# A two-layer hybrid block: rounded weights' products first, ada pieces moved, GLA roots by ScalarE, mLSTM chain ahead of a low part

## The reference, cut to what matters

```python
for layer in range(DEPTH):
    mod = (silu(c) @ ada_w[layer] + ada_b[layer])[:, None, :]
    sh_m, sc_m, g_m, sh_f, sc_f, g_f = jnp.split(mod, 6, axis=-1)
    h = rms_norm(x, norm_w[layer, 0]) * (1.0 + sc_m) + sh_m
    y = even_mixer(h, ...) if layer % 2 == 0 else odd_mixer(h, ...)
    x = x + g_m * rms_norm(y, norm_w[layer, 1])
    h = rms_norm(x, norm_w[layer, 2]) * (1.0 + sc_f) + sh_f
    y = conv_ffn(h, ffn_in_w[layer], ffn_conv_w[layer], ffn_conv_b[layer], ffn_out_w[layer])
    x = x + g_f * rms_norm(y, norm_w[layer, 3])

def odd_mixer(h, w_in, a_w2, a_b, g_norm_w, w_out):
    ...
    o = rms_norm(gla(...), g_norm_w.reshape(G_HEADS, G_DV))
    return (o * silu(gr)).reshape(b, t, -1) @ w_out
```

## Time and profile before

| | us |
|---|---|
| median of three runs | 2381.96 (2379.38 to 2383.01) |
| the profiled execution | 2381.75 |
| its span, first to last instruction | 2379.7 |
| TensorE busy | 2336.1 (98%) |
| VectorE busy | 2001.0 (84%) |
| ScalarE busy | 1052.4 (44%) |
| DMA, mean over the span | 263 GB/s |

### The profile page before, as it was taken

The page is one execution under the profiler, slowest core; times in us unless marked ns, Lnnn a source line. Parts: engine busy times, 40 slices in busy tenths (PEclk is TensorE's granted clock), DMA queues, the critical chain, the costliest instruction groups (busy, mean ns, idle before and its releaser), DMA issues.

```text
span 2379.7 us, 32710 instructions
## 1 busy us (share of the span) xinstructions
PE 2336.1 (98%) x12512; PEld 2005.1 (84%) x12512; DVE 2001.0 (84%) x2821; ACT 1052.4 (44%) x1181; POOL 15.8 (1%) x22
## 2 busy tenths in 40 slices
PE   8999999999999999999999999999999999999998
PEld 7789898788878888888888888888888888888886
DVE  7779998999989999999888778888887688877875
ACT  2144545544434444344465554655434343433343
POOL 0000010000000000000000000000000000000000
PEclk9999999999999999999999999999999999999999
DMA  9999977677799778977848545385556755576553
GB/s 393 413 395 370 378 260 284 245 257 260 263 376 348 265 257 299 395 261 259 330 181 314 198 171 184 142 338 192 180 191 225 288 198 189 194 275 233 182 194 142
DMA packets 114766, 625.73 MB, mean 263 GB/s; under 512 B 12801, under 2 KB 13249, under 8 KB 63441
## 3 DMA queue, kind: packets, MB, share of 16 engines
q1 hardware_dynamic: 113938, 619.81, 70.1%
q10 hardware_dynamic: 704, 4.23, 0.5%
HBM read 621.85 MB, written 2.13 MB: 262 GB/s over the span
## 4 chain that ended last, share of the span: by engine, by line
PE 79%; DVE 10%; DMA 7%; ACT 3%; issue 1%; DVEq 0%; ACTq 0%
PE bank L2152 32%; PE bank L2154 17%; PE bank L2179 8%; PE bank L2181 8%; PE bank L2180 8%; DMA region<-ada_pieces 5%; DVE lo L1132 4%; DMA piece<-ada_pieces 1%; DVE region L1155 1%; ACT hi L644 1%; PE bank L2149 1%; PE bank L2150 1%; DVE piece L1155 1%; PE bank L2058 1%; PE bank L1908 0%
## 5 line engine op out<-in xcount | busy, mean ns | idle before, releaser
L2152 PE MATMUL bank<-act,hi 128*128 128x512 f32 x3328 | 1048.2, 396 | 4.3 <-DVE act L1217 2.9
L644 ACT ACTIVATE hi<-raw 128x2048 fp32r<-128x2048 f32 x375 | 717.9, 1914 | 753.3 <-PE bank L2181 387.6
L1132 DVE TENSOR_TENSOR lo<-raw,hi 128x2048 fp32r<-128x2048 f32 x375 | 857.6, 2287 | 128.2 <-ACT hi L644 127.7
L2154 PEld LDWEIGHTS bank<-act,lo 128*128 128x128 f32 x3616 | 670.0, 188 | 147.5
L2154 PE MATMUL bank<-act,lo 128*128 128x256 f32 x3616 | 711.9, 278 | 0.0
L2152 PEld LDWEIGHTS bank<-act,hi 128*128 128x128 f32 x3328 | 506.9, 189 | 6.5 <-DVE act L1217 3.3
L2179 PE MATMUL bank<-hi,mid 128*128 128x512 f32 x704 | 274.9, 391 | 1.6 <-DVE lo L1132 1.6
L2180 PE MATMUL bank<-lo,mid 128*128 128x512 f32 x704 | 274.0, 389 | 0.0
L2181 PE MATMUL bank<-hi,mid 128*128 128x512 f32 x704 | 274.0, 389 | 0.0
L1155 DVE SCALAR_TENSOR_TENSOR piece<-piece,cond 128x1024 f32<-128x1024 f32 x207 | 250.8, 1218 | 12.4 <-DMA piece<-ada_pieces 12.3
L2179 PE MATMUL bank<-hi,act 128*128 128x512 f32 x512 | 203.5, 398 | 5.5 <-DVE lo L1132 4.5
(11 more groups left out here) (215 smaller groups left out, 1834.5 us busy)
## 6 DMA issues: line engine op xcount, KB each, us to landing
raw<-w_units SPq DMA_DIRECT2D x378, 1024.0 KB, 4.8
piece<-ada_pieces SPq DMA_DIRECT2D x207, 512.0 KB, 5.6
region<-ada_pieces SPq DMA_DIRECT2D x137, 512.0 KB, 8.0
raw<-head_units SPq DMA_DIRECT2D x16, 1024.0 KB, 16.0
y<-ada_pieces SPq DMA_DIRECT2D x30, 512.0 KB, 6.7
extra<-ada_pieces SPq DMA_DIRECT2D x10, 512.0 KB, 5.8
region<-gamma_scratch ACTq DMA_DIRECT2D x4, 1024.0 KB, 7.4
x<-x_in SPq DMA_DIRECT2D x2, 1024.0 KB, 6.1
```

The lines of the kernel that those rows point to most:

```text
L644: sc.activation(hi[:, slot, :], raw[:, raw_slot, :], ACT.Copy).then_inc(s_hi, 1)
L1132: ve.tensor_tensor(lo[:, slot, :], raw[:, raw_slot, :], hi[:, slot, :].bitcast(F32), ALU.subtract).then_inc(s_lo, 1)
L2152: pe.matmul(both, w, act[:, k, :], start=k == 0, stop=False)
L2154: i_ = pe.matmul(dst, w, act[:, k, 0:T], start=False, stop=k == DK - 1)
```

## The change

- TensorE waits for `hi` before a unit and forms all its products with the high part of the weight first; then it waits for `lo` (`rest_ready`) and forms the others. In a phase's last unit, which is summed block by block, this holds for each block.
- In the mLSTM columns VectorE runs `after_split` (the head chain) ahead of the next unit's low part.
- In the norm the low part of the phase's second unit goes behind the last two activation parts (`low(6)`, `low(7)`).
- Ada pieces move: (2, 2, 2, 2) to (1, 2, 2, 3) in the mLSTM columns, two pieces from layer 0's second ff_down to layer 1's mixed phase.
- GLA: ScalarE takes the inverse root by `Ln` and `Exp(-0.5 x)` from the bank; VectorE's mean and reciprocal are gone. A root that loads ScalarE's table for the norm is also taken in mixed phases, at unit 6.

```diff
--- before
+++ after
@@ -110,19 +110,19 @@
               Phase("values", 0, 1, 8, (3, 2) * 4, side="fox", side0=2, ring=EARLY),
-              Phase("columns", 0, 2, 4, (2,) * 4, dest=MO, side="mlstm"),
+              Phase("columns", 0, 2, 4, (1, 2, 2, 3), dest=MO, side="mlstm"),
               Phase("mixed", 0, 1, 16, (0, 0, 0, 1, 1, 2, 2, 2, 1, 2, 2, 2, 2, 1, 1, 0), ring=(0, 1, ROWS)),
...
               Phase("ff_up", 0, 8, 4, (1, 1, 1, 0), 1, ring=(0, 1, GAMMA)),
-              Phase("ff_down", 0, 1, 16, (2, 2, 2, 2, 2, 3, 2, 2, 2, 2, 2, 2, 2, 2, 2, 2), 1, ring=(0, 1, GAMMA, GAMMA + 1)),
+              Phase("ff_down", 0, 1, 16, (2,) * 15 + (1,), 1, ring=(0, 1, GAMMA, GAMMA + 1)),
               Phase("ff_up", 0, 6, 4, (1, 1, 1, 0), 2, ring=(0, 1, GAMMA)),
...
               Phase("columns", 1, 2, 8, (0,) * 8, dest=GR, side="gla", side0=2),
-              Phase("mixed", 1, 1, 16, (0, 0, 1, 0, 1, 2, 2, 2, 1, 1, 3, 2, 3, 1, 1, 0), ring=HEADS + (0, 1)),
+              Phase("mixed", 1, 1, 16, (0, 0, 1, 1, 2, 2, 2, 2, 1, 1, 3, 2, 3, 1, 1, 0), ring=HEADS + (0, 1)),
               Phase("ff_up", 1, 8, 4, no, 0), Phase("ff_down", 1, 1, 16, (1,) * 16, 0),
@@ -665,6 +665,12 @@
                 sc.activation(at_, at_, ACT.Sqrt, bias=bias, scale=scale).then_inc(s_root, 1)
+
+            def inverse_root(at_, sums, scale, bias, logs):
+
+                sc.activation(at_, sums, ACT.Ln, bias=bias, scale=scale).then_inc(s[logs[0]], 1)
+                sc.wait_ge(*(s[logs[0]], logs[1]))
+                return sc.activation(at_, at_, ACT.Exp, scale=-0.5)
 
@@ -909,8 +915,9 @@
 
-                sc.wait_ge(s["gla_mean_ready"], heads)
-                sc.activation(g_rstd, g_rstd, ACT.Sqrt, scale=float(G_DK)).then_inc(s["gla_root_ready"], 1)
+                sc.wait_ge(s["gla_squares_summed"], heads)
+                inverse_root(g_rstd, bank[5][:, T:2 * T], 1.0 / G_DV, stat[:, S_KEPS:S_KEPS + 1], ("gla_mean_ready", heads))\
+                  .then_inc(s["gla_rstd_ready"], 1)
 
@@ -1058,7 +1065,7 @@
                         if ph.sums:
-                            if ph.kind == "ff_down" and j == 1:
+                            if j == (1 if ph.kind == "ff_down" else 6):
                                 sc.activation(stat[:, S_WARM:S_WARM + 1], stat[:, S_EPS:S_EPS + 1], ACT.Sqrt)
@@ -1238,9 +1245,9 @@
                     low(p)
-                split_next(ph, 0, 0)
                 low(6)
                 low(7)
+                split_next(ph, 0, 0)
 
@@ -1536,31 +1543,16 @@
                     if not first_body(h):
-                        if j == 1:
-                            gla_mean(h)
-                        if j == 2:
-                            gla_inverse(h)
                         if j in (3, 4):
...
 
-            def gla_mean(heads):
-
-                ve.wait_ge(s["gla_squares_summed"], heads)
-                ve.tensor_scalar(g_rstd, bank[5][:, T:2 * T], 1.0 / (G_DV * G_DK), EPS, ALU.mult, ALU.add)\
-                  .then_inc(s["gla_mean_ready"], 1)
-
             def gla_add_squares(heads):
...
                   .then_inc(s["gla_squares_added"], 1)
-
-            def gla_inverse(heads):
-
-                ve.wait_ge(s["gla_root_ready"], heads)
-                ve.reciprocal(g_rstd, g_rstd).then_inc(s["gla_rstd_ready"], 1)
 
@@ -1662,10 +1654,7 @@
                         low_part(ph, 2)
-                    if j == 2:
-                        gla_mean(G_HEADS)
                     if j == 3:
-                        gla_inverse(G_HEADS)
                         gla_normed(G_HEADS, 0)
@@ -1673,6 +1662,7 @@
 
+            ve.memset(stat[:, S_KEPS:S_KEPS + 1], EPS * G_DK)
             ve.memset(stat[:, S_EPS:S_EPS + 1], EPS).then_inc(s_v, own.tick())
@@ -1771,9 +1761,12 @@
                         before_split(ph, i, j)
+                        if ph.side == "mlstm":
+                            after_split(ph, i, j)
                         if not (ph.norms and first_body(i) and j == 0):
                             split_next(ph, i, j)
-                        after_split(ph, i, j)
+                        if ph.side != "mlstm":
+                            after_split(ph, i, j)
                         if ph.kind == "values" and ph.layer == 0 and ph.side is None and j == 1:
@@ -2127,6 +2120,9 @@
                     i_.then_inc(s["gate_transposed"], 1)
+                def rest_ready(ph, i, j):
+                    pe.wait_ge(s_lo, RAW_SLOTS + unit(ph, i, j) + 1)
+
                 def columns(ph, i, j, slot):
@@ -2143,15 +2139,15 @@
                         w_hi = [hi[:, slot, k * P:(k + 1) * P] for k in two]
-                        w_lo = [lo[:, slot, k * P:(k + 1) * P] for k in two]
                         for k, w in zip(two, w_hi):
...
                                 pe.matmul(both, w, act[:, k, :], start=k == 0, stop=False)
-                        for k, w in zip(two, w_lo):
-                            i_ = pe.matmul(dst, w, act[:, k, 0:T], start=False, stop=k == DK - 1)
+                    rest_ready(ph, i, j)
+                    for k in range(DK):
+                        i_ = pe.matmul(dst, lo[:, slot, k * P:(k + 1) * P], act[:, k, 0:T], start=False, stop=k == DK - 1)
                     return i_
@@ -2164,29 +2160,31 @@
                     by_blocks = ph.sums and j == ph.units - 1
-                    order = [(q, tb) for tb in range(TB) for q in range(4)] if by_blocks else \
-                        [(q, tb) for q in range(4) for tb in range(TB)]
-                    for q, tb in order:
-                        kt = 4 * group + q
-                        if tb == 0 and ph.kind == "ff_down" and first_body(i) and tile == 0:
-                            pe.wait_ge(s_mid, ph.pairs - FF_GROUPS[ph.group] + kt + 1)
-                        if tb == 0 and ph.side == "gla" and q == 2:
-                            gla_midway(ph, i, j)
-                        w_hi, w_lo = hi[:, slot, q * 512:(q + 1) * 512], lo[:, slot, q * 512:(q + 1) * 512]
-                        dst = bank[2 * (tile_no % 2) + tb][:, :]
-                        x_hi = src[:, kt, tb * P:(tb + 1) * P]
-                        x_lo = src[:, kt, T + tb * P:T + (tb + 1) * P]
-                        pe.matmul(dst, x_hi, w_hi, start=opens and q == 0, stop=False)
-                        pe.matmul(dst, x_hi, w_lo, start=False, stop=False)
-                        i_ = pe.matmul(dst, x_lo, w_hi, start=False, stop=closes and q == 3)
-                        if by_blocks and (q, tb) == (3, 0):
+                    for blocks_of in ((0,), (1,)) if by_blocks else ((0, 1),):
+                        for q in range(4):
+                            for tb in blocks_of:
+                                kt = 4 * group + q
+                                if tb == 0 and ph.kind == "ff_down" and first_body(i) and tile == 0:
+                                    pe.wait_ge(s_mid, ph.pairs - FF_GROUPS[ph.group] + kt + 1)
+                                if tb == 0 and ph.side == "gla" and q == 2:
+                                    gla_midway(ph, i, j)
+                                w_hi = hi[:, slot, q * 512:(q + 1) * 512]
+                                dst = bank[2 * (tile_no % 2) + tb][:, :]
+                                pe.matmul(dst, src[:, kt, tb * P:(tb + 1) * P], w_hi, start=opens and q == 0, stop=False)
+                                pe.matmul(dst, src[:, kt, T + tb * P:T + (tb + 1) * P], w_hi, start=False, stop=False)
+                        rest_ready(ph, i, j)
+                        for q in range(4):
+                            for tb in blocks_of:
+                                i_ = pe.matmul(bank[2 * (tile_no % 2) + tb][:, :], src[:, 4 * group + q, tb * P:(tb + 1) * P],
+                                               lo[:, slot, q * 512:(q + 1) * 512], start=False, stop=closes and q == 3)
+                        if by_blocks and blocks_of == (0,):
                             i_.then_inc(s_first, 1)
...
                         slot = (ph.n0 + j) % SPLIT_SLOTS
-                        pe.wait_ge(s_lo, RAW_SLOTS + unit(ph, i, j) + 1)
+                        pe.wait_ge(s_hi, unit(ph, i, j) + 1)
                         (tokens if ph.tokens else columns)(ph, i, j, slot).then_inc(s_unit, 1)
```

4 lines of the change are left out of this document (2 added, 2 removed).

## The result

The changed kernel takes 2386.27 us in the median of sixteen runs (2384.42 to 2389.70), the kernel before, on the same chip, 2381.76 (2377.68 to 2386.81). The ratio is 1.002, its 95% interval 1.0013 to 1.0026: slower by 4.5 us, a small difference, but the interval leaves out 1. The forecast was 2376.4, faster, with a range up to 2386.0; both the sign and the range were missed. The profiled execution has 2387.2 us and a span of 2385.4, 5.7 more than that of before.

The account below looks back on a forecast made before the run. TensorE, busy for 98% of the span, was taken as the bound, so time could come only from its waits or matmul spacing. 2381.75 with -10.9 - 4.6 + 3.7 + 6.5 = -5.3 gave 2376.4 us, range 2366 to 2386.

Parts of the forecast that it names:

- High products first: TensorE's fifteen waits for low parts, 12.4 us, go, about 1.5 stays: 10.9 us gained (bounds 7 to 12.4).
- Uniform spacing: Matmuls grouped by width in ff_up and layer 1's columns: 0.022 us gained in each of 208 units, 4.6 us.
- rival C: Matmul spacing doesn't change with the order of widths: 2381.0 us, no change; chance 18%.
- First units after norms: Three units, sixteen low products now behind the last pair: 1.2 us lost each, 3.7 in all (bounds 2 to 4.5).
- mLSTM columns: Head chain moved and pieces redealt, with a cold clock behind: 6.5 us lost (bounds 1.6 gained to 9.5 lost).
- Two round trips of the ring: mLSTM columns, second body: pieces wait for reloads in two slots; mixed phase starts 5 us late.
- the chain's new place: mLSTM columns, second body: with the head chain ahead of the low part, TensorE goes on 1.2 us earlier.
- rival B: mLSTM columns: third pieces wait for nothing, clock stays up; term -1.6 instead of +6.5, 2368.3 us; chance 22%.
- The clock: TensorE, idle some 6 us before the first mixed phase, starts cold: about 1.5 us lost.
- The rest: GLA roots, warming root and two pieces moved from ff_down to the second mixed phase: zero (bounds -1 to +1.5).
- The sum: Whole kernel: -10.9 - 4.6 + 3.7 + 6.5 = -5.3 us, from 2381.75 to 2376.4.

Follow-up runs that it names:

- run 10: Changed kernel without its two mLSTM column edits, low products threaded after norms, one piece moved from unit 14 to 2 of the first mixed phase: 2370.53 us.
- run 1: Changed kernel with two pieces in every unit of the mLSTM columns again, head chain still ahead of the low part: 2380.05 us.
- Run 7: Changed kernel with low products threaded between the pairs in the three first units after a norm: 2381.10 us.
- Run 3: Kernel before with only the head chain put ahead of the low part in the mLSTM columns: 2388.52 us.
- run 4: Kernel before with only the mLSTM columns' pieces dealt out as (1, 2, 2, 3): 2388.34 us.
- run 2: Changed kernel with the low part ahead of the head chain again in the mLSTM columns, pieces as changed: 2382.11 us.
- run 5: Changed kernel without its two mLSTM column edits (two pieces in every unit, low part ahead of the chain): 2375.63 us.
- Run 11: Kernel before with only the GLA roots, the warming root and the two pieces moved into the second mixed phase: 2379.90 us.

## Why the prediction was wrong, point by point

**High products first: right, returns mis-sized.** Forecast -10.9 with 1.5 us given back. The traces show 1.6 + 2.4 + 8.6 = 12.6 us of waits gone for 12.4 forecast, and 2.3 given back at the end of the first mixed phase: -10.3, within the bounds. TensorE comes to the last unit earlier, VectorE doesn't (run 10 shows what it was doing; in run 1's trace only 0.3 came back). The second mixed phase, with the same edit, gave nothing back.

**Uniform spacing: wrong, rival C held in its size.** Forecast -4.6; the steady unit went from 5.573 to 5.567 us, 1.2 us in the sum of the phases. TensorE's rows of one such unit (start, duration, count), from two narrow windows and a wide one:

```profile
861.71 1.78 PE L2147 MATMUL bank<-act,hi 128*128 128x512 f32 x7
...
863.09 2.43 PE L2147 MATMUL bank<-act,hi 128*128 128x512 f32 x10
...
861.71 3.82 PE L2147 MATMUL bank<-act,hi 128*128 128x512 f32 x16
...
865.36 2.08 PE L2150 MATMUL bank<-act,lo 128*128 128x256 f32 x16
...
867.27 1.09 PE L2147 MATMUL bank<-act,hi 128*128 128x512 f32 x4
```

The seventh 512-wide product starts at 863.09, six starts after 861.71 (0.230 each), and ten starts later, at 865.36, the 256-wide ones begin (0.227 each). Start to start, the first five distances are 233, 236, 228, 233 and 231 ns, the others 226 to 227. So the run of sixteen takes 3.65 us, not 3.627, and the sixteen 256-wide ones 1.91: the first two of their distances are 113 and 119 ns, the others 120. In the kernel before every 512-wide product was among these first ones (0.233 each), and the 256-wide ones between them took 0.114 to 0.117. My step set both widths to their pure pace and left 1 ns for the changes of width in a unit; they cost 20.
The Trainium skill (TensorE: Matmul & The Clock Gate, "Back-to-back issue gap") has a formula for the gap that knows the width alone, and calls it the gap of an isolated matmul. In these rows the pace depends on what ran before as well, though for the sum the formula's outcome, no gain, was nearer than mine.

**First units after norms: right, but for the clock.** Forecast +1.2 each, 3.7 in all. They cost 1.26, 1.22 and 2.68, 5.2 in all, of which 1.4 is the clock in layer 1. (A slip of 0.03 in the working, 477.42 + 0.69 is 478.11, changes nothing.) Run 7 shows that the cause is the place of the low products, and that the norm's new order is worth 0.3 us each as soon as they are threaded.

**mLSTM columns: the mechanism half right, and the step that failed.** Forecast +6.5, with 9.5 as the worst; measured 8.0 in the columns and 1.3 behind them. Two round trips of the ring, as forecast: loads issued at 362.00 and 369.59, waited for until 368.33 and 373.30. But I counted the chain's new place as a gain of 1.2 us for TensorE, and as the whole of rival B (-1.6). Run 3 puts it at +5.2 us in the columns. This is the step that failed. The sentence "with the chain first it waits for ScalarE's exponentials instead" names the wait and then prices it for TensorE alone. It is VectorE that waits there, 1.0 to 1.2 us for each chain, with the low part that filled this time now behind it. The four chains of the changed kernel make 4.5 us of it, as in run 3; the 3.3 us for which VectorE had waited for TensorE in these columns are too few to take in this and the longer waits for pieces, so everything behind moves. I had it finish the second unit's chain at 346.2; the trace has 349.9 (348.9 with this execution's later start taken off), and TensorE went on behind it 1.6 us later, counted from the start of the columns, not 1.2 earlier. The pieces stand in my sum with 6.2 us of the columns (the 5 and the chain's 1.2); they cost 4.1 in run 4 and 5.8 in run 2 against run 5. Rival B, at 22%, fails on its own condition: in run 4 a third piece waits 1.77 us even in the old order.

**The clock.** Forecast 1.5 us behind the columns; the first mixed unit takes 7.64 us where it takes 6.22 to 6.24 at full clock, 1.4.

**The rest.** Zero forecast; GLA's phases differ by +0.1 us between the traces. Run 11 shows a gain of its own that does not add to that of the new order.

**The sum.** Forecast -5.3, the spans +5.7. The 11.0 between them: spacing 3.4, mLSTM 2.8, the fox columns 2.6, which no edit explains, first units 1.5, the hi-first term 0.6, and 0.1 of the rest. The hi-first term and the mLSTM term lie within their bounds, the first units 0.7 outside, but all erred to the same side, and the range allowed for one of them at a time. As a term of the sum the spacing is off the most; the largest single mistake is the sign of the chain's move: -1.2 in the sum, +3.7 (changed against run 2), +4.6 (run 1 against run 5) or +5.2 (run 3) in the columns, by what stands around it. The mLSTM term shows only 2.8 us of it, because the pieces cost less than I had put and the two edits overlap. The medians, from two chips, split in the same way: without the two mLSTM edits (run 5) the change is worth -6.7 us where the other terms sum to -11.8, and the two edits cost 10.6 us where the term is 6.5.

## What to carry to other kernels

Before an instruction is moved ahead of another on an engine that has little slack, look at what its input waits for: the one that is jumped over may have been the cover of that wait, and the price is the cover's loss on this engine, not the consumer's gain on the other. When waits for a late operand are taken away by using it last, look for the places where the other operand is what comes late (here the first unit after a norm): there it should be used as it comes. And a ring of two slots punishes uneven work: a third piece in one unit waits for a load that went out only when the piece two before it was summed (1.8 to 2.3 us of waiting here).

## What the runs showed of the hardware

The clock of TensorE differs between executions of the same instructions. Behind the waits of 0.73 and 0.84 us in the first unit after a norm it stayed at 1.00 in layer 0 and stood at 0.66 over the next window in layer 1, within one execution. Behind the wait of 3.31 us in the mLSTM columns the unit took 12.31 us in the kernel before (clock 0.72 in the window of the wait) and 10.92 in run 5 (1.00). Most such falls cost about 1.4 us. In the first mixed unit it was 1.4 us behind the wait of 8.59 (7.64 against 6.23) and more behind shorter ones: 2.6 us in run 2 (3.98 us of wait), 2.8 in run 7 (7.23), 2.3 in run 4 (3.72, against 6.78). Part of the scatter of about 2 us about each median may be of this kind; that share was not measured.

The pace of a matmul is not a function of its width alone: the first five 512-wide ones behind 256-wide ones start 228 to 236 ns apart, the others 226 to 227; 256-wide ones start 120 ns apart in their own run, after two distances of 113 and 119, and take 114 to 117 between 512-wide ones.
